# A two-mixer decoder trunk on one core: both mixers group by group, or the first for all groups and then the second

## The chip, the cores and the metric

The kernel runs on one core of a Trainium2 chip. The metric is the device time of one execution in microseconds (us). TensorE is called PE, VectorE DVE, ScalarE ACT, GpSimd POOL, and SyncE, which issues most transfers, SP.

## What is computed

The input is x, 2048 tokens of 1024 features in float32. There are two layers, each with RMS norm, a shift, scale and gate from a conditioning vector, and a residual:

```
h = rms_norm(x) * (1 + scale) + shift
u, v, z = split(h @ w_in)                    # first mixer, 3 x 2048 columns
y = gelu(u) * (w_s[causal] @ layer_norm(gelu(v)) + b_s) * silu(z)   # chunks of 128 tokens, 8 column groups
x1 = x + gate * (y @ w_out)
k, v = split(rms_norm(x1) * kv_norm @ w_kv)  # 2 heads of 64, k rotated
q, z = split((rms_norm(x1) * (1 + scale) + shift) @ w_in_b)         # 16 heads of 64, q rotated
o = softmax(q k^T / 8, window of 128, a learned sink per head) v
out = rms_norm(x1 + gate * ((o * silu(z)) @ w_out_b)) * final_norm
```

Attention works on blocks of 128 queries against this block and the one before it.

## The kernel before

The tokens are cut into four groups of 512 (`group(i)`), and a group's 512 tokens are four chunks of 128. A group goes through both mixers before the next begins; group 0 is written out and the others run in a loop (`groups`), on every engine.

**Numbers in halves.** All large products are made from a rounded high part and a remainder: high x high, high x low, low x high, three matmuls for one (`split3`, L1329 to L1331). For weights ACT rounds (`hi`, L615) and POOL subtracts (`lo`, L508); for activations ACT rounds and DVE subtracts.

**Units and pieces.** The weights stream from HBM in units of 4 x 128 rows by 512 columns, into two buffers in turn; each unit arrives as two halves. A group has 44 units: 8 for v (`U_V`), 16 for u and z in eight slabs (`U_UZ`), 8 for the first output projection (`U_AO`), 4 for q, 4 for z, 4 for the second output projection (`U_BO`). A unit is eight pieces of six matmuls with 512 columns. `piece_done` counts pieces, and SP loads the unit after next into a buffer when its pieces are done.

**First mixer.** v is projected and its statistics taken; then each slab projects u and z, DVE forms `vs`, PE does the spatial matmuls (L1472), DVE gates (L1090 to L1115). Then y is split (`y_rest`) and projected. In group 0 DVE also makes the rotary tables (`table`, 17 operations on 128x512) between the y remainders, ACT takes their sines, and they go through HBM.

**Second mixer.** x1 is normalised and turned by PE (`x1_transposes`), copied, multiplied out to K and V, and the modulated `hb` is made by DVE and split. q is rotated: ACT copies a bank with its halves swapped (L660, four instructions), DVE multiplies by cosine and sine and adds (`rope`, L1006 to L1009), ACT rounds (L673, L674), DVE takes the remainder (L1019, L1020). The order is swap 0, swap 1, out 0, swap 2, out 1 and so on (`Q_BEFORE`). Attention is 16 steps, each four heads of one block:

```python
FILLERS = [4, 3, 2] + [2] * 4 + [3] * 9
```

is the number of projection pieces that PE does in each step; four more stand ahead (`AHEAD`). A step: logits (L1583, into two banks that all steps share); DVE masks and takes the maximum (L1245 to L1258); ACT exponentials (L855); DVE adds the sink, takes the reciprocal (L1267, L1269); POOL scales (L573); PE transposes (L1592, one step later, into bank 6); ACT and DVE split (L849, L1263); POOL makes the masked copy (L567); PE multiplies with V (L1604, three steps later, into bank 7); ACT and DVE combine it (L867, L1275). When a tile of o is whole, DVE gates it (L1033). Then come the output projection, the residual (`residual`, L1147 and L1151), the last norm (L1317) and the store. The next group's x is scaled, turned (L1359) and split beside the output projection.

The order on every queue is written out by hand: an engine that waits holds up all that stands behind it.

## Time and profile before

| | |
|---|---|
| three runs | 2602.76, 2607.14, 2607.95 us |
| median | 2607.14 us |
| profiled execution, span from first to last instruction | 2608.2 us |
| busy: PE, DVE, POOL, ACT | 90%, 55%, 46%, 41% |
| transfers | 250 MB, mean 96 GB/s |

The span is that of one profiled execution. No time of it outside the span is given; it lies within 0.3 us of the slowest run. PE's busy time counts overlapping matmuls once, and a busy PE need not run at its full clock; the granted clock is given as a share of 2.4 GHz, in which 0.5 is 1.2 GHz.

### The profile page before, as it was taken

How to read it: one execution, taken by the hardware profiler on the slowest of the kernel's cores; microseconds unless marked ns; L12 is line 12 of the kernel's file. 1: busy time of each engine (PE TensorE's matmuls, PEld its weight loads, DVE VectorE, ACT ScalarE, POOL GpSimd, SP SyncE). 2: the span in 40 equal slices, each digit the busy share in tenths (PEclk: the TensorE clock that was granted, in tenths of full speed). 3: DMA queues.
4: the chain of work that ended last, by engine and by line, in shares of the span. 5: the costliest groups of instructions: out<-in, count | busy, mean ns of one | idle time of the engine just before them, and what ended most of it. 6: DMA issues, size and time to landing. Idle time of an engine off the chain costs nothing.

```text
span 2608.2 us, 31861 instructions
## 1 busy us (share of the span) xinstructions
PE 2341.7 (90%) x10725; PEld 1929.0 (74%) x10725; DVE 1443.3 (55%) x1885; ACT 1057.6 (41%) x1979; POOL 1187.1 (46%) x597
## 2 busy tenths in 40 slices
PE   4999997878899999887889999987898999998787
PEld 3878885656688888776678888876677888886566
DVE  6645477678533443568651444267854254436784
ACT  3222232655442223365453222347544222236552
POOL 3344343255554444435645444524654444452564
PEclk9999998988899999998999999998999999998998
DMA  7642232211232224211223222421133322322112
GB/s 268 238 172 89 88 129 85 74 36 41 105 129 89 89 88 138 89 49 33 97 74 129 91 88 88 136 73 49 41 105 106 97 89 88 129 97 65 41 33 89
DMA packets 151955, 250.04 MB, mean 96 GB/s; under 512 B 9408, under 2 KB 80160, under 8 KB 151712
## 3 DMA queue, kind: packets, MB, share of 16 engines
q1 hardware_dynamic: 147104, 234.94, 27.3%
q10 hardware_dynamic: 4736, 13.67, 1.3%
q8 instruction: 60, 0.98, 0.1%
...
## 4 chain that ended last, share of the span: by engine, by line
issue 28%; PE 21%; POOL 17%; DVE 16%; ACT 8%; DVEq 6%; DMA 2%; POOLq 2%; ACTq 0%; SPq 0%
POOL w_lo L508 16%; PE ps L1329 6%; PE ps L1330 6%; PE ps L1331 6%; DVEq L1247 4%; ACT pp L855 3%; DVE es L1267 3%; ACT zb L660 2%; DVE mx L1252 2%; DVE ob L1033 1%; DVE negm L1255 1%; DVE zb L1006 1%; DVEq L1008 1%; POOLq L515 1%; DVE ps L1245 1%
## 5 line engine op out<-in xcount | busy, mean ns | idle before, releaser
L508 POOL TENSOR_TENSOR w_lo<-w_raw,w_hi 128x1024 fp32r<-128x1024 f32 x352 | 879.5, 2511 | 1061.6 <-ACT w_hi L615 1061.1
L615 ACT ACTIVATE w_hi<-w_raw 128x1024 fp32r<-128x1024 f32 x352 | 370.1, 1059 | 798.3 <-DMA w_raw<-in_a_w_in 577.4
L1329 PE MATMUL ps<-hb,w_hi 128*128 128x512 f32 x512 | 213.7, 417 | 23.1 <-DVE zb L1006 22.1
L567 POOL TENSOR_TENSOR pt<-pt,keep 128x1024 fp32r<-128x1024 f32 x64 | 152.3, 2380 | 174.1 <-DVE pt L1263 174.1
L1329 PE MATMUL ps<-w_hi,y_hl 128*128 128x512 f32 x512 | 202.8, 396 | 22.5 <-POOL w_lo L508 22.5
L1101 DVE SCALAR_TENSOR_TENSOR wz<-wz,ps 128x512 f32<-128x512 f32 x64 | 43.6, 687 | 315.8 <-ACT wz L733 315.8
L1330 PE MATMUL ps<-hb,w_hi 128*128 128x512 f32 x512 | 209.8, 410 | 0.0
L1331 PE MATMUL ps<-hb,w_lo 128*128 128x512 f32 x512 | 208.7, 408 | 0.0
L1329 PE MATMUL ps<-h_low,w_hi 128*128 128x512 f32 x512 | 202.6, 396 | 6.3 <-ACT vy L705 3.6
L1330 PE MATMUL ps<-w_lo,y_hl 128*128 128x512 f32 x512 | 201.3, 393 | 0.0
L1331 PE MATMUL ps<-w_hi,y_hl 128*128 128x512 f32 x512 | 201.0, 393 | 0.0
L1331 PE MATMUL ps<-h_low,w_lo 128*128 128x512 f32 x512 | 200.1, 391 | 0.0
L1330 PE MATMUL ps<-h_low,w_hi 128*128 128x512 f32 x512 | 200.0, 391 | 0.0
L1329 PE MATMUL ps<-h_high,w_hi 128*128 128x512 f32 x512 | 199.2, 389 | 0.0
L1330 PE MATMUL ps<-h_high,w_hi 128*128 128x512 f32 x512 | 199.2, 389 | 0.0
L1331 PE MATMUL ps<-h_high,w_lo 128*128 128x512 f32 x512 | 199.2, 389 | 0.0
L1123 DVE TENSOR_TENSOR y_hl<-vy,y_hl 128x512 fp32r<-128x512 f32 x64 | 77.5, 1269 | 169.3 <-ACT y_hl L745 169.2
L855 ACT ACTIVATE pp<-ps,negm 128x128 f32<-128x128 f32 x256 | 90.7, 366 | 188.7 <-DVE negm L1255 188.7
...
L1329 PEld LDWEIGHTS ps<-hb,w_hi 128*128 128x128 f32 x512 | 103.2, 202 | 49.7 <-DVE zb L1006 28.6
L1592 PE MATMUL ps<-ident,pp 128*128 128x128 f32 x256 | 44.7, 303 | 99.7 <-DVE pt L1263 99.6
L1329 PEld LDWEIGHTS ps<-w_hi,y_hl 128*128 128x128 f32 x512 | 97.3, 190 | 44.5 <-issue 20.5
...
## 6 DMA issues: line engine op xcount, KB each, us to landing
w_raw<-in_a_w_in SPq DMA_DIRECT2D x256, 256.0 KB, 2.8
...
```

Source lines behind the costliest of these rows:

```text
L508: g.tensor_tensor(wlo[p][:, rows_], raw[p][:, rows_], whi[p][:, rows_].bitcast(F32), ALU.subtract).then_inc(w_lo, 1)
L567: g.tensor_tensor(pt[:, k % 2, 2:4].rearrange("p a (h q) -> p (a h) q", h=4), pt[:, k % 2, 0:2].bitcast(F32).rearrange("p a (h q) -> p (a ...
L615: s.activation(whi[p][:, rows_], raw[p][:, rows_], ACT.Copy).then_inc(w_hi, 1)
L660: last = s.activation(zb[32 * q:32 * q + 32, 2 * (n % 2), :], ps[o:o + 32, 512 * b:512 * b + 512], ACT.Copy)
L855: last = s.activation(pp[:, st % 2, h, :], ps[:, 2048 + 256 * h + P:2048 + 256 * h + 2 * P], ACT.Exp, bias=negm[:, st % 2, h:h + 1], scale ...
L1123: v.tensor_tensor(y[:, t % 4, 1, :], vy[:, T * t:T * t + T], y[:, t % 4, 0, :].bitcast(F32), ALU.subtract).then_inc(y_lo, 1)
L1247: dve.drain()
L1252: v.tensor_reduce(mx[:, slot, :], both[:, :, P:2 * P], AXIS_X, ALU.max)
L1267: v.tensor_tensor(es[:, slot, :], es[:, slot, :], psum_[:, slot, :], ALU.add)
L1329: t_.matmul(dst, stat[0], mov[0], start=start, stop=False)
L1330: t_.matmul(dst, stat[0], mov[1], start=False, stop=False)
L1331: return t_.matmul(dst, stat[1], mov[0], start=False, stop=stop)
```

## The change

The four groups go through the first mixer one after the other; the next group's x is now turned beside the last unit of the first output projection. Each group's x1 is stored in HBM (`x1_kept`); it is scaled and turned by PE one tile after each slab of the next group, copied by ACT and stored as well (`x1_turned`). The rotary tables are made after slabs 0 to 3 of group 0.

Then a second phase runs the second mixer of all groups. Its weight units stand in one list: K/V, q and z of the first eight heads for group 0; then, for each group i, q and z of the other eight heads, the output projection of group i-1, and K/V, q and z of the first eight heads of group i+1; last the output projection of group 3. The 416 pieces of the 52 units are dealt out over slots: 8 slots without attention, 64 slots with one attention step each, 8 slots at the end. The probabilities are transposed after the first piece of the next slot and multiplied with V after its fourth; the transposes and the products now share bank 6. DVE gates o in every step, and the gated, split output goes through HBM (`oz_kept`) except for group 3. K/V's input is scaled from the stored turned tile by ACT and its remainder taken by DVE (`xk_round`, `xk_rest`); `hb` is made by ACT from the same tile during the K/V unit, whose weights are now an ordinary unit without kv_norm in them. Weights of a later unit are split on ACT and POOL two pieces after their buffer is free. All loops are written out. The residual keeps its product in the PSUM bank.

The core of the diff, by engine:

```diff
-UNITS = 44
-PIECES = 8 * UNITS
-U_V, U_UZ, U_AO, U_Q, U_Z, U_BO = 0, 8, 24, 32, 36, 40
-STEPS = 16
+U_V, U_UZ, U_AO, A_UNITS = 0, 8, 24, 32
+FIRST_B = A_UNITS * NG
+def b_order():
+    units, starts = [], []
+    def kv_q0_z0(g):
+        units.append(("kv", g, 0, 0))
+        for kind in "qz":
+            for ku in range(2):
+                units.append((kind, g, 0, ku))
+    starts.append(0)
+    kv_q0_z0(0)
+    for i in range(NG):
+        starts.append(len(units))
+        for kind in "qz":
+            for ku in range(2):
+                units.append((kind, i, 1, ku))
+        if i >= 1:
+            for n in range(2):
+                for ku in range(2):
+                    units.append(("b", i - 1, n, ku))
+        if i < NG - 1:
+            kv_q0_z0(i + 1)
+    starts.append(len(units))
+    for ku in range(2):
+        for n in range(2):
+            units.append(("b", NG - 1, n, ku))
+    return units, starts + [len(units)]
+PRO_SLOTS, STEPS, TAIL_SLOTS = 8, 16, 8
+def b_slots():
+    slots = []
+    for it, count in enumerate([PRO_SLOTS] + [STEPS] * NG + [TAIL_SLOTS]):
+        first, n = 8 * B_STARTS[it], 8 * (B_STARTS[it + 1] - B_STARTS[it])
+        for s in range(count):
+            slots.append(range(first + n * s // count, first + n * (s + 1) // count))
+    return slots
+def by_halves(u):
+    if u < FIRST_B:
+        return u % 2 == 0 and u % A_UNITS != U_AO + 6
+    kind, g, n, ku = B_UNITS[u - FIRST_B]
+    return kind == "kv" or ku == 0 or (kind == "b" and n == 1 and g < NG - 1)
+def freed(u, hh):
+    return 4 + 4 * hh if by_halves(u) else 8
+AFTER_FREE = 2
+def weights_at(pc):
+    found = []
+    for u in range(FIRST_B + 2, UNITS):
+        for hh in range(2):
+            if 8 * (u - 2 - FIRST_B) + freed(u - 2, hh) - 1 + AFTER_FREE == pc:
+                found.append((u, hh))
+    return found
...
+        x1d = nc.dram_tensor("x1_kept", [NG, P, NC, D], F32).ap()
+        xtd = nc.dram_tensor("x1_turned", [NG, KT, P, T], F32).ap()
+        ozd = nc.dram_tensor("oz_kept", [NG - 1, KT, P, 2, T], F32).ap()
...
 sync
+            def keep_turned(i, kt):
+                sp.wait_ge(t1_copied, at("t1_copied", i, kt + 1))
+                sp.dma_start(xtd[i, kt], xst[:, kt % 2, :]).then_inc(xt_out[kt % 2], 16)
...
+                for g in range(GROUPS + 1):
+                    unit(first + U_UZ + 2 * g)
+                    unit(first + U_UZ + 2 * g + 1)
+                    if i >= 1 and g >= 1:
+                        keep_turned(i - 1, g - 1)
...
+            def load_oz(g, half):
+                done = B_AT[("z", g + 1, 1, half)]
+                sp.wait_ge(piece_done, b_pieces(8 * done + 8))
+                for n in range(2):
+                    sp.wait_ge(oz_out[n], 16 * (4 * g + 2 * half + 2))
+                sp.dma_start(r[:, 4 * half:4 * half + 4].bitcast(F32),
+                             ozd[g, 4 * half:4 * half + 4].rearrange("k p a t -> p k a t")).then_inc(oz_in[half], 16)
...
 gpsimd
+            for s, slot in enumerate(SLOTS):
+                a = s - PRO_SLOTS
+                for k, pc in enumerate(slot):
+                    tasks(pc)
+                    if k == 0:
+                        if 0 <= a - 1 < ATT:
+                            mask(a - 1)
+                        if 0 <= a < ATT:
+                            normalise(a)
...
 scalar
+            def hb_round(g, kt):
+                act.wait_ge(piece_done, b_pieces(8 * B_AT[("kv", g, 0, 0)] + kt + 1))
...
+                for dst_ in (hfx[:, kt % 2, :], r[:, kt, 0, :]):
+                    last = s_.activation(dst_, xin[:, kt, :], ACT.Identity, bias=sb_[:, kt:kt + 1],
+                                         scale=gb[:, kt:kt + 1])
...
+            def tasks(pc):
+                kind, g, n, ku, k = unit_of(pc)
...
+                kind2, g2, n2, ku2, k2 = unit_of(pc - 2)
+                if kind2 == "q" and ku2 == 1 and k2 % 2 == 1:
+                    m = 4 * n2 + k2 // 2
+                    act.wait_ge(roped, at("roped", g2, m + 1))
...
+                    s_.activation(qs[0:64, 2 * m, :], whole[0:64, :], ACT.Copy)
+                    s_.activation(qs[64:P, 2 * m + 1, :], whole[64:P, :], ACT.Copy).then_inc(q_hi, 1)
+                if kind == "q" and ku == 1 and k % 2 == 1:
...
+                    swap_from(m % 4, zb[2 * (m % 2)], swapped)
...
+                for u, hh in weights_at(pc):
+                    hi(u, (hh,))
+                if kind == "kv":
+                    hb_round(g, k)
...
 vector
+                for g in range(GROUPS - 1):
+                    uz_group(g)
+                    if i == 0 and g < NG:
+                        table(g)
+                    if g == 2 and i < NG - 1:
+                        x_scale(i + 1)
...
+            def residual(x_, b, cnk, n, gate, read):
+                dve.drain()
+                v.tensor_tensor(bank(b), bank(b), gate[:, 512 * n:512 * n + 512], ALU.mult)
+                dve.drain()
+                v.tensor_tensor(x_[:, cnk, 512 * n:512 * n + 512], x_[:, cnk, 512 * n:512 * n + 512], bank(b),
+                                ALU.add).then_inc(read, 1)
...
+                for k, pc in enumerate(slot):
+                    tasks(pc)
+                    if k == 0:
+                        if 0 <= a < ATT:
+                            dve.wait_ge(sink_exp, a + 1)
+                            v.tensor_tensor(es[:, at_, :], es[:, at_, :], psum_[:, at_, :], ALU.add)
+                            dve.drain()
+                            v.reciprocal(rden[:, at_, :], es[:, at_, :]).then_inc(r_ready, 1)
...
+                    if k == min(3, len(slot) - 1) and 0 <= a - 1 < ATT:
...
+                        v.tensor_tensor(obt[0:64], high[:, :, 0, :], ot[0:64], ALU.add)
+                        v.tensor_tensor(obt[64:P], high[:, :, 1, :], ot[64:P], ALU.add)
+                        dve.drain()
+                        gated = zg[:, f0:f0 + 2, P * blk:P * blk + P]
+                        v.scalar_tensor_tensor(gated, obt[:], 0.5, gated, ALU.mult, ALU.mult).then_inc(o_done, 1)
...
 tensor
-                for f in range(AHEAD):
-                    filler(f)
-                for st in range(STEPS):
-                    f = AHEAD + sum(FILLERS[:st])
-                    logits(st)
-                    filler(f)
-                    if st >= 3:
-                        values(st - 3)
-                    filler(f + 1)
-                    for k in range(2, FILLERS[st]):
-                        filler(f + k)
-                    if st >= 1:
-                        p_transposes(st - 1)
+            for s, slot in enumerate(SLOTS):
+                a = s - PRO_SLOTS
+                if 0 <= a < ATT:
+                    logits(a)
+                for k, pc in enumerate(slot):
+                    b_piece(pc)
+                    kind, g, _, _, kk = unit_of(pc - 2)
+                    if kind == "kv" and kk == 7:
+                        k_transposes(g)
+                    if 24 <= pc < 24 + KT:
+                        x1_transposes(NG - 1, pc - 24, 4 + pc % 2)
+                    if k == 0 and 0 <= a - 1 < ATT:
+                        p_transposes(a - 1)
+                    if k == min(3, len(slot) - 1) and 0 <= a - 1 < ATT:
+                        values(a - 1)
```

## Rows read from the trace of the kernel before

**Rows 1.** The page, engines over the whole span: busy us (share) xinstructions.

```profile
PE 2341.7 (90%) x10725; PEld 1929.0 (74%) x10725; DVE 1443.3 (55%) x1885; ACT 1057.6 (41%) x1979; POOL 1187.1 (46%) x597
```

**Rows 2.** Stretches: busy us of each engine, then granted clock, DMA share, GB/s.

```profile
54.30:460.50 406.20, 383.01 (x1729) 316.20 (x1728) 239.19 (x278) 115.23 (x146) 162.26 (x68) 0.97 0.39 132
...
723.40:1091.00 367.60, 364.72 (x1677) 303.50 (x1676) 143.70 (x171) 115.67 (x148) 172.52 (x78) 1.00 0.33 106
1091.00:1351.00 260.00, 213.64 (x986) 173.70 (x984) 186.76 (x266) 147.32 (x345) 121.64 (x64) 0.91 0.19 61
...
2349.00:2608.20 259.20, 205.07 (x954) 164.19 (x952) 180.23 (x264) 136.84 (x331) 119.66 (x68) 0.92 0.17 57
```

**Rows 3.** Stretches of group 1's second mixer; columns as before.

```profile
1150.30:1293.30 143.00, 116.71 (x521) 93.25 (x520) 116.03 (x179) 81.70 (x239) 81.40 (x43) 0.89 0.15 47
```

**Rows 4.** Waits of PE, 1091 to 1351 us: total, times, longest.

```profile
PE ps L1592 <- DVE pt L1263: 23.4, 9, 5.1
...
PE ps L1329 <- DVE zb L1006: 5.8, 4, 2.0
```

**Rows 5.** Timeline of PE, dense matmuls: start us, us, instruction.

```profile
1348.11 0.39 PE L1329 MATMUL ps<-w_hi,oz 128*128 128x512 f32 x1
...
1350.15 0.39 PE L1329 MATMUL ps<-w_hi,oz 128*128 128x512 f32 x1
```

**Rows 6.** Timeline inside an attention step, all engines.

```profile
1234.70 2.40 POOL L567 TENSOR_TENSOR pt<-pt,keep 128x1024 fp32r<-128x1024 f32 x1 [2.88 <-DVE pt L1263]
...
1235.28 0.60 PE L1592 MATMUL ps<-ident,pp 128*128 128x128 f32 x4
...
1235.44 1.68 DVE L1267 TENSOR_TENSOR es<-es,psum__137 128x4 f32<-128x4 f32 x1 [0.81 <-ACT es L860]
...
1236.66 0.39 PE L1329 MATMUL ps<-hb,w_hi 128*128 128x512 f32 x1
```

**Rows 7.** DVE groups, one row a shape: busy us, mean ns | idle before.

```profile
L1009 DVE TENSOR_TENSOR zb<-zb 128x512 f32<-128x512 f32 x36 | 41.0, 1140 | 2.7
...
L1020 DVE TENSOR_TENSOR qs<-zb,qs 64x512 fp32r<-64x512 f32 x32 | 38.8, 1214 | 0.4
...
L1007 DVE TENSOR_TENSOR zb<-zb,cs 128x512 f32<-128x512 f32 x36 | 29.8, 828 | 0.0
...
L1182 DVE TENSOR_TENSOR kvn<-xt,kvn 128x512 fp32r<-128x512 f32 x32 | 29.2, 953 | 10.1 <-ACT kvn L791 10.1
...
L1006 DVE TENSOR_TENSOR zb<-ps,cs 128x512 f32<-128x512 f32 x36 | 24.9, 692 | 51.8 <-ACT zb L660 50.5 <-issue 1.0
...
L1019 DVE TENSOR_TENSOR qs<-zb,qs 64x512 fp32r<-64x512 f32 x32 | 24.2, 757 | 2.9
L1317 DVE SCALAR_TENSOR_TENSOR x<-x,r,fn 128x1024 f32<-128x1024 f32 x16 | 22.5, 1417 | 25.0 <-POOL r L516 25.0
```

**Rows 8.** ACT groups, columns as in the group above.

```profile
L615 ACT ACTIVATE w_hi<-w_raw 128x1024 fp32r<-128x1024 f32 x352 | 370.1, 1059 | 798.3 <-DMA w_raw<-in_a_w_in 577.4 <-DMA w_raw<-in_a_w_out 190.6 <-DMA w_raw<-in_b_w_out 24.0
...
L660 ACT ACTIVATE zb<-ps 32x512 f32<-32x512 f32 x144 | 84.9, 589 | 2.4 <-PE ps L1528 0.2
...
L673 ACT ACTIVATE qs<-zb 64x512 fp32r<-64x512 f32 x32 | 20.2, 631 | 5.7 <-DVE zb L1009 5.2
```

**Rows 9.** POOL groups, columns the same.

```profile
L508 POOL TENSOR_TENSOR w_lo<-w_raw,w_hi 128x1024 fp32r<-128x1024 f32 x352 | 879.5, 2511 | 1061.6 <-ACT w_hi L615 1061.1 <-issue 0.2
```

**Rows 10.** PE groups, columns the same.

```profile
L1359 PE MATMUL ps<-ident,xs 128*128 128x128 f32 x128 | 24.5, 364 | 25.3 <-DVE bt L1147 22.4 <-ACT h_low L638 2.8
```

**Rows 11.** Waits of PE in group 0's first mixer.

```profile
PE ps L1329 <- POOL w_lo L508: 19.8, 2, 13.9
```

**Rows 12.** Timeline of DVE, half of one rotary table.

```profile
412.23 0.43 DVE L978 TENSOR_SCALAR tab<-tab 128x512 f32<-128x512 f32 x1
...
416.55 0.43 DVE L992 TENSOR_SCALAR tabo<-tab 128x512 f32<-128x512 f32 x1
```

**Rows 13.** Timeline of PE, the last matmul of the kernel.

```profile
2597.95 0.39 PE L1331 MATMUL ps<-w_hi,oz 128*128 128x512 f32 x1
```

1867 lines of the change are left out of this document (922 added, 945 removed).

## Prediction

> **What bounds the kernel now.** I read the engines' totals first. PE is busy 90% of the span [rows 1], and no other engine is over 55%. That share hides two kinds of stretch. Cut at the first matmul of each stage, the span is 54.3 us of start, a first mixer of 406.2 us (group 0), three of about 367.6, and four second mixers that share the rest: 2608.2 - 54.3 - 406.2 - 3 x 367.6 = 1044.9 us, about 261 each [rows 2]. In a first mixer PE is busy for 364.7 of 367.6 us at a granted clock of 1.00. In a second mixer it is busy 213.6 of 260.0 at 0.91, and DVE is busy 186.8, which is 72%.
>
> The price of PE's work comes from starts, not from durations, since matmuls overlap: nine 512-column matmuls start in 2.04 us, so one costs 0.227 us [rows 5]. A piece (six of them) is 1.37 us, a unit (eight pieces) 10.9. An attention step adds four transposes and eight logits matmuls, 1.38 us from 1235.28 to 1236.66 [rows 6], and four value matmuls, 0.91: 2.3 us. The first mixer is thus at its PE floor (32 units are 349 us, the spatial matmuls make up most of the rest). The second is not: 12 units 131, 16 steps 37, K/V 11, transposes about 7, together 186 of 261 us.
>
> What holds it is in the sixteen steps: 143.0 us, 8.9 us a step, DVE busy 116.0 (81%), PE clock 0.89 [rows 3]. Step work of PE is 2.3 plus 2.25 projection pieces, 5.4 us. The longest wait of PE in group 1's whole second mixer is that of the probability transposes for DVE's split of the step before, 23.4 us in 9 waits, and 5.8 us go to rope, ahead of the steps [rows 4]. So a second mixer is a cross-engine chain with DVE nearly full, and pieces between its links are too few.
>
> **The change part by part.** First mixer, groups 1 to 3: same units. PE now also turns the next x (24.5/4 = 6.1 us by its busy time [rows 10], which overlaps; I take 4) and the kept x1 (the same number of transposes, 4). Their copies on ACT and the scale on DVE lie in a stage where ACT is busy 115.7 and DVE 143.7 of 367.6 us [rows 2]; if that cover were gone they would cost about 2 us for each of eight tiles. That gives 375, 375, and 371 for group 3, which turns no next x. SP now waits for each turned tile between weight loads, behind it stands the next unit's load; it waits only for a copy that is due early in the slab, so nothing is charged.
>
> Group 0: 19.8 us of waiting for w_lo go [rows 11], whose root is ACT standing in its queue for the tables that DVE makes. The tables move between DVE's slab work. One table is two halves of 16 operations in all; one half takes 4.75 us without company [rows 12], so about 10, up to 14 where POOL is in the way. DVE is free for 61% of a first mixer [rows 2], 14 us of a slab's 23.6, but the table stands between one slab's gating and the next one's `vs`, for which PE's spatial matmuls wait; in slab 2 the scaling of the next x (four operations on 128x1024, 1.4 each like L1317 [rows 7]) is added. I charge 2 us for three slabs and 9 for slab 2, 15 in all, and take 5 off for the clock that the old wait had lowered (0.97 in the row). 406.2 - 19.8 - 5 + 15 + 4 = 400. The four: 1521. If the tables hide, 1506; if each comes in full, 1545.
>
> Second mixers: the work is now 416 pieces and 64 steps: 40 pieces in 8 slots before the first step, then 72, 104, 104 and 64 pieces over 16 steps each, then 32 pieces in 8 slots. PE's floor for the four is 72 x 1.37 + 37 = 136, 180, 180, 125: 620 us (old steps had 36 pieces for 16). Start: 55 + 4 for the last x1 transposes; tail: 44.
>
> DVE's load. The old steps' 116.0 us hold four ropes of 0.69 + 0.83 + 1.14 = 2.66, four q remainders of 1.97, eight z gates of 0.69 (they read PSUM, as rope's first operation does), and four output gates with remainders, 6.5 [rows 7]. 85.5 are left, 5.3 a step. New in each step is the gating of 128x256 from SBUF, which no row shows; between 0.35 (half of L1006's 512 columns) and 0.95 (L1182), I take 0.65: 6.0 a step, 95 for 16. Around them per group: eight ropes and K's 24, q remainders 16, z gates 5.5, output remainders 5.5, second residual 8 x 1.44 (now both operations read PSUM) 11.5, final scale 4 x 1.42, xk remainders 8 x 0.95, hb remainders 5.5, K/V about 6. Put where they fall, the four iterations hold 162, 179, 179 and 142 us: 662. Gone from DVE there are x1's normalisation, the whole hb (ACT makes it from the stored tile), half the K/V splits, and both x stages. So DVE has more than PE, 662 against 620. The engines are level, and the time is set by how well the queues mesh.
>
> Two ways to size it. By fill: at the 81% of the old steps, 662/0.81 = 817. By stalls on PE, which are 620 plus:
> - Rope. ACT's order is now: q high parts of column m-1 (which wait for its rope), then the swap of m. A column is 4 x 0.59 swap [rows 8] + 2.66 rope + 2 x 0.63 = 6.3 us in series against 2.74 for PE's two pieces. The fourth bank is read 3 x 6.3 + 2.4 + 0.7 = 22 us after the first is full; PE wants it after nine pieces and one to two steps, 15 us. At least 7, and with a step's DVE work in between up to 20. I take 14, seven times: 98. Queued behind ACT's wait are the exponentials and w_hi, and PE's next logits and weights wait for those.
> - K/V units: two activations per piece on ACT for hb, 1.3 of 1.37 us, beside a step's 3 us: 7, three times, 21.
> - Mask: after the transposes come a copy on ACT (0.6, as L673) [rows 8], DVE's remainder (0.7, as L1006) [rows 7] and POOL's 2.4 [rows 6], 3.9 us with the hand-overs against three pieces, 4.1. It fits unless POOL has just begun a 2.5 us weight half [rows 9]; 0.5 a step, 32.
>
> That is 771. I take 800. Start with one rope stage unhidden: 71. Tail: PE's last matmul stands 10 us before the old end [rows 13], the same chain follows here, and the last step drains in it: 57. Extra transfers (x1 and its turned copy out and in, the gated output of three groups) are hidden: the queues are used 17 to 19% in these stretches [rows 2]. ACT takes up new weights two pieces after the buffer is free, 2.7 us, and may stand a microsecond for them; that is within the 30 between the two ways. SP passes these stores and loads between weight loads; behind a 2 MB load one weight half comes late by some 6 us, which has twelve pieces of slack.
>
> Sum: 54 + 1521 + 71 + 800 + 57 = 2503 against the profiled 2608.2. The runs' median lies 1 us under that span: about 2502.
>
> A rule is weighed here. In a step, DVE's 4-element sum of `es` takes 1.68 us and ends at 1237.12, with POOL's mask at 1237.10 [rows 6]. The Trainium skill (SBUF — State Buffer, Who interferes with whom) says that a DVE instruction with two SBUF inputs is fully blocked while a GpSimd instruction reads SBUF. The trace agrees. By that rule the new gating and xk operations wait too, and POOL's share in iterations 1 and 2 (an old step's 3.4, which is 81.4 less 11 weight halves over 16, so 16 x 3.4 + 26 halves x 2.5 = 120 of some 210 us) is no higher than the 57% of the old steps [rows 3], so the mean durations used above carry over. At a full mask wait for every new gating, 2.4 instead of 0.65, it would be 64 x 1.75 = 112 us more, 2614.
>
> **The rivals.** (1) The chain hides and PE sets the time: mask and K/V stalls alone, 620 + 53 = 673 for the slots, start 60, tail 54: 2362, up to 2430 with half the rope stalls. For: slots of 4.5 to 6.5 pieces where 2.25 stood, and PE reached 1.00 wherever it was fed. Against: DVE's 662 alone, and waits in fixed order.
> (2) Slower: the in-order coupling lets DVE fill only as it does over a whole old second mixer, 72% [rows 2]: 662/0.72 = 919, and 54 + 1521 + 71 + 919 + 57 = 2622. It decides from 905 us in the slots, a fill of 73%, or 14.1 us a slot. For: the rope chain in series, in which ACT, then DVE, then PE stand. Against: old stretches at 72% held stages with no step to run beside them (normalisation, output projection); here they overlap.
> (3) No change: the gain is exactly eaten, the slots at 895 to 905.
>
> **How the numbers follow.** 0.2% (5 us) is about what a measurement of this kernel can tell from no change. Forecast, slots 740 to 890, 2440 to 2590: 0.64. Rival 1: 0.20. Rival 2, with what lies between it and the forecast: 0.14. Rival 3: 0.02. Range: 2395 (between rival 1's two values) to 2605; about 0.1 is left out on each side. Faster 0.86, same 0.02, slower 0.12.
>
> **What would show it.** First mixers of 371 to 376 us, group 0 near 400 with waits of spatial matmuls for `vs` and no 13.9 us wait for w_lo. Sixteen-step stretches near 175, 226, 226 and 173 us, DVE above 75% busy, PE's clock above 0.91 except at q stages; PE waiting for rope's first product at z's first pieces, 10 us and more at a time; transposes waiting for DVE's gating or for exponentials. Wrong if the slots are nearly PE's floor with few rope waits (rival 1), if DVE is under 73% busy there and ACT stands for rope (rival 2), or if weights arrive late behind SP's new waits.

## The result and the profile after

The change makes the kernel slower. The kernel after takes 2634.7 us (median of four runs, 2633.7 to 2638.2), the kernel before beside it 2606.0 (2602.8 to 2608.0): ratio 1.0118, 95% interval 1.0100 to 1.0136. Forecast were 2502 us, 2395 to 2605 and a faster kernel: the time lies outside the range and on the other side. Below, a run's time is the median of its fast executions, since one execution of one kernel (`e16_rest_later`) fell in a slower state and took 2988.7 us.

The engine totals of the kernel after hardly differ from those of before [rows 1]:

```profile
PE 2323.3 (88%) x10725; PEld 1919.2 (73%) x10725; DVE 1436.3 (55%) x1900; ACT 1076.8 (41%) x2018; POOL 1171.0 (44%) x573
```

Stretches of the kernel after, cut where its stages begin: four first mixers, the start of the second phase up to the first logits, the four iterations of sixteen slots, and the tail. The columns are those of [rows 2].

```profile
54.30:459.00 404.70, 394.37 (x1809) 326.22 (x1808) 244.13 (x287) 135.16 (x176) 165.41 (x68) 1.00 0.43 145
459.00:828.00 369.00, 368.27 (x1720) 307.41 (x1719) 147.91 (x173) 125.57 (x167) 163.61 (x70) 1.00 0.35 116
...
1568.00:1651.50 83.50, 53.81 (x228) 43.26 (x229) 31.27 (x42) 45.87 (x75) 20.74 (x10) 0.82 0.22 70
1651.50:1867.70 216.20, 154.32 (x734) 125.36 (x733) 154.25 (x242) 125.79 (x314) 100.88 (x49) 0.90 0.21 71
1867.70:2133.80 266.10, 205.28 (x934) 167.63 (x933) 182.67 (x271) 139.42 (x334) 125.49 (x66) 0.89 0.31 109
2133.80:2400.00 266.20, 210.43 (x934) 172.21 (x933) 184.53 (x268) 139.43 (x334) 125.54 (x66) 0.87 0.31 109
2400.00:2575.70 175.70, 138.61 (x647) 109.33 (x645) 135.93 (x211) 89.91 (x253) 99.83 (x51) 0.93 0.31 108
2575.70:2632.90 57.20, 45.32 (x194) 37.02 (x194) 30.21 (x34) 14.53 (x24) 23.58 (x21) 0.91 0.31 111
```

The first phase is full: PE is busy 368 of 369 us, at a clock of 1.00. The deviation lies behind it. The 64 slots take 216.2 + 266.1 + 266.2 + 175.7 = 924.2 us where 800 were forecast, and DVE is busy 657.4 of them, 71%. The last iteration, which holds one rotary stage and no K/V unit, takes 175.7 us for the 173 of the forecast; the other three, with two rotary stages and a K/V unit each, take 40 us more than forecast apiece. PE's longest waits in the slots of the kernel after, and two of ACT's (time, number of waits, longest):

```profile
PE ps L1603 <- POOL pt L675: 101.8, 46, 7.0
PE ps L1596 <- DVE zg L1390: 68.0, 27, 11.1
PE ps L1399 <- DVE zb L1243: 15.5, 6, 5.4
PE ps L1399 <- DVE x L1114: 13.2, 8, 2.9
PE ps L1399 <- ACT vf L917: 11.3, 2, 5.7
```

```profile
...
ACT qs L931 <- DVE zb L1246: 64.8, 25, 4.3
...
ACT w_hi L717 <- DMA w_raw<-in_b_w_in: 26.7, 7, 9.3
```

PE seldom waits for the rope itself (15.5 us). It waits for the mask (L675, by the value products L1603) and for the gating (L1390, by the transposes L1596), which stand on POOL and DVE behind everything else. These names tell who was last, not why. So I sorted the slots: from each step's logits to the next, against PE's price as the prediction has it, 1.37 us a piece and 2.3 a step. A slot is called K/V if it holds a piece of a K/V unit, rotary if it or the four pieces ahead of it hold a piece of a q unit's second half (there the columns become ready), other if neither.

| 63 slots, us | rotary (23) | K/V (8) | other (32) |
|---|---|---|---|
| PE's price | 225.5 | 85.5 | 299.6 |
| kernel after | 412.4 | 148.5 | 351.3 |
| over the price | 186.8 | 63.0 | 51.7 |
| of this PE idle | 134.0 | 42.1 | 37.2 |
| PE busy beyond its price | 52.8 | 20.9 | 14.5 |
| mean granted clock | 0.83 | 0.84 | 0.98 |

The other slots run near the price: iteration 1's slots 4 to 8 take 10.7 to 12.0 us. The rotary ones do not: its slots 1 to 3 take 20.2, 18.4 and 25.0.

The excess is not all waiting. Slots 1 to 3 and then 4 to 8 of iteration 1, and around one wait in slot 15 (columns as above):

```profile
1878.40:1942.00 63.60, 41.89 (x170) 33.26 (x169) 42.66 (x59) 30.52 (x70) 26.07 (x12) 0.84 0.26 96
1942.00:2000.20 58.20, 56.31 (x273) 46.10 (x272) 38.75 (x64) 28.17 (x77) 37.08 (x18) 1.00 0.49 172
...
2122.70:2127.05 4.35, 0.02 (x2) 0.04 (x1) 0.68 (x1) 0.00 (x0) 4.35 (x3) 1.00 0.00 0
2127.40:2130.80 3.40, 3.40 (x10) 2.66 (x9) 1.09 (x3) 0.76 (x2) 0.50 (x1) 0.50 0.00 0
2131.00:2134.00 3.00, 3.00 (x16) 2.49 (x15) 0.69 (x1) 0.65 (x2) 0.00 (x0) 1.00 0.00 0
```

At a granted clock of 1.00 PE is busy 56.3 us for work whose price is 55.3; at 0.84 it is busy 41.9 for 34.3. In the third stretch PE stands and the clock is still at 1.00; in the fourth it is at 0.50 (1.2 GHz), and 128x512 matmuls that otherwise start 0.23 us apart start 0.43 apart; in the fifth it is back. So a wait of PE is paid twice here, once as idle time and once in the slower matmuls behind it. Over the 64 slots PE is busy 708.6 us for a price of 620 and idle 215.6.

### The profile page after: what moved, and what is told of

It is laid out like the page before. It is cut to its first block, busy times and chain, and to the rows that moved or that the text cites. A ratio compares the mean times of both kernels' runs of the same rounds, so it can differ in the third digit from the quotient of the medians.

```text
span 2632.9 us, 28491 instructions
## 1 busy us (share of the span) xinstructions
PE 2323.3 (88%) x10725; PEld 1919.2 (73%) x10725; DVE 1436.3 (55%) x1900; ACT 1076.8 (41%) x2018; POOL 1171.0 (44%) x573
## 4 chain that ended last, share of the span: by engine, by line
PE 63%; DVE 14%; ACT 7%; DVEq 5%; DMA 4%; issue 4%; POOL 3%; SPq 0%; POOLq 0%; ACTq 0%
PE ps L1399 19%; PE ps L1400 19%; PE ps L1401 19%; POOL pt L675 2%; ACT zb L872 2%; PE ps L1549 2%; DVEq L1351 2%; DMA w_raw<-in_b_w_in 1%; DVEq L1245 1%; DVE zb L1246 1%; ACT pp L994 1%; DVE mx L1356 1%; DVE zb L1243 1%; DVEq L1388 1%; DVE es L1371 1%
## 5 line engine op out<-in xcount | busy, mean ns | idle before, releaser
L1399 PE MATMUL ps<-h,w_hi 128*128 128x512 f32 x1024 | 401.9, 392 | 0.0
L1401 PE MATMUL ps<-h,w_lo 128*128 128x512 f32 x1024 | 398.8, 389 | 0.0
L1400 PE MATMUL ps<-h,w_hi 128*128 128x512 f32 x1024 | 398.6, 389 | 0.0
L1399 PE MATMUL ps<-r,w_hi 128*128 128x512 f32 x512 | 224.4, 438 | 46.3 <-ACT vf L917 25.8
L675 POOL TENSOR_TENSOR pt<-pt,keep 128x1024 fp32r<-128x1024 f32 x64 | 156.8, 2451 | 224.8 <-DVE pt L1365 224.8
L1401 PEld LDWEIGHTS ps<-h,w_lo 128*128 128x128 f32 x1024 | 192.3, 188 | 40.6
L1399 PEld LDWEIGHTS ps<-h,w_hi 128*128 128x128 f32 x1024 | 192.4, 188 | 39.4 <-POOL w_lo L618 0.4
L1400 PEld LDWEIGHTS ps<-h,w_hi 128*128 128x128 f32 x1024 | 192.5, 188 | 39.3
L1400 PE MATMUL ps<-r,w_hi 128*128 128x512 f32 x512 | 215.8, 421 | 0.0
L1401 PE MATMUL ps<-r,w_lo 128*128 128x512 f32 x512 | 213.4, 417 | 0.0
L1399 PE MATMUL ps<-w_hi,h 128*128 128x512 f32 x512 | 201.2, 393 | 1.9 <-POOL w_lo L618 1.9
L1401 PE MATMUL ps<-w_hi,h 128*128 128x512 f32 x512 | 200.0, 391 | 0.0
L1400 PE MATMUL ps<-w_lo,h 128*128 128x512 f32 x512 | 200.0, 391 | 0.0
L1129 DVE BATCH_NORM_STATS2 stats<-vy 128x6 f32<-128x512 f32 x64 | 42.6, 689 | 231.5 <-ACT vy L774 231.4
L1399 PEld LDWEIGHTS ps<-r,w_hi 128*128 128x128 f32 x512 | 108.0, 211 | 70.1 <-issue 26.4
```

Source lines behind the costliest of these rows:

```text
L675: g.tensor_tensor(pt[:, 2:4].rearrange("p a (h q) -> p (a h) q", h=4), pt[:, 0:2].bitcast(F32).rearrange("p a (h q) -> p (a h) q", h=4), k ...
L1129: v.bn_stats(stats[:, cnk, j, :], src[:, :, cnk, :])
L1399: t_.matmul(dst_, stat[0], mov[0], start=start, stop=False)
L1400: t_.matmul(dst_, stat[0], mov[1], start=False, stop=False)
L1401: return t_.matmul(dst_, stat[1], mov[0], start=False, stop=stop)
```

## The experiments

Eighteen runs. Each ratio is to the kernel before on the same chip, with its 95% interval. The theories of the first four runs are A, the rope chain in series on ACT; B, DVE has too much work in whatever order; C, weights come late; D, the bank shared by transposes and products is freed late.

### The rope chain on ACT: the swap first, and the same made worse in the kernel before

`e1_swap_first`, on the kernel after: ACT swaps column m before it rounds column m-1, which waits for DVE's rope.

```diff
-                if kind2 == "q" and ku2 == 1 and k2 % 2 == 1:
-                    ...   # wait for rope m-1, round it to qs
                 if kind == "q" and ku == 1 and k % 2 == 1:
                     ...
                     swap_from(m % 4, zb[2 * (m % 2)], swapped)
+                if kind2 == "q" and ku2 == 1 and k2 % 2 == 1:
+                    ...   # wait for rope m-1, round it to qs
```

> The changed kernel with one order turned round on ScalarE: the half-swap of q column m stands ahead of the rounding of column m-1, which waits for VectorE's rope of m-1. Same instructions, same load. Theory A (the rope chain in series: swap 2.4, rope 2.7, rounding 1.3 us per column, with an attention step's work caught behind it): a column drops from 6.3 to about 3.7 us, seven stages in the slots win 7 to 10 us each and the one ahead of them 8: 2550 to 2575 us. Theory B (VectorE simply has too much work for the slots, in whatever order): no more than 10 us, 2625 to 2635. Theory C (weights come late) and theory D (the bank that transposes and value products share is freed late) expect no change either.

Measured: 2599.3 us, ratio 0.9982 (0.9968 to 0.9996), 35 us less than the kernel after. The direction is theory A's, the gain about half of the 60 to 85 us that it expected. The excess of the rotary slots fell from 186.8 to 153.9, the start of the second phase shortened as well (the first logits came 9.7 us earlier), and the other slots stayed (57.2).

The timeline of the kernel after shows the series that this cuts. In brackets is the idle time before an instruction, and who ended it. First DVE, then ACT in the same stretch:

```profile
1897.79 0.69 DVE L1246 TENSOR_TENSOR zb<-zb,zb 128x512 f32<-128x512 f32 x1
1902.30 0.69 DVE L1243 TENSOR_TENSOR zb<-ps,cs 128x512 f32<-128x512 f32 x1 [3.82 <-ACT zb L872]
...
1905.87 0.70 DVE L1349 COPY_PREDICATED ps<-prev,ps 128x512 f32<-128x512 uint32 x1
...
1907.74 0.68 DVE L1365 TENSOR_TENSOR pt<-ps,pt 128x512 fp32r<-128x512 f32 x1
```

```profile
1898.52 0.63 ACT L931 ACTIVATE qs<-zb 64x512 fp32r<-64x512 f32 x1 [3.83 <-DVE zb L1246]
1899.16 0.63 ACT L932 ACTIVATE qs<-zb 64x512 fp32r<-64x512 f32 x1
1899.81 2.39 ACT L872 ACTIVATE zb<-ps 32x512 f32<-32x512 f32 x4
```

ACT stands 3.83 us for DVE's rope, then DVE 3.82 us for ACT's swap: each idles while the other works. DVE's softmax (L1349) and its remainder of the probabilities (L1365) stand in line behind, so the wait reaches PE under the mask's name.

`b1_serial_before` gives the kernel before the same serial order.

```diff
-Q_BEFORE = (("in", 0), ("in", 1), ("out", 0), ("in", 2), ("out", 1), ("in", 3), ("out", 2), ("out", 3))
+Q_BEFORE = (("in", 0), ("out", 0), ("in", 1), ("out", 1), ("in", 2), ("out", 2), ("in", 3), ("out", 3))
```

> The kernel before, with the four q columns ahead of its attention steps in the changed kernel's order (swap 0, rounding 0, swap 1, rounding 1 and so on). Theory A: a column goes from 3.7 to about 6 us, so three columns in each of four groups cost 5 to 10 us a group, 20 to 40 us: 2628 to 2648. Theory B: VectorE has little to do there, no change beyond 5 us.

Measured: 2637.9 us, ratio 1.0127 (1.0105 to 1.0148): 33 us more, as theory A expected. That one order costs as much in either kernel, so the change, beside all else, had given up an order on ACT worth as much as its whole loss against the kernel before.

### The shared bank: two tries, no effect

`e2_bank_release`, on the kernel after: the bank counts as free once DVE has read it (`obt`), not once the output is gated.

```diff
-                        v.tensor_tensor(obt[64:P], high[:, :, 1, :], ot[64:P], ALU.add)
+                        v.tensor_tensor(obt[64:P], high[:, :, 1, :], ot[64:P], ALU.add).then_inc(o_read, 1)
...
-                    pe.wait_ge(o_done, a)
+                    pe.wait_ge(o_read, a)
```

> The changed kernel with a separate semaphore that frees the shared bank after the two additions that read it, instead of after the gating behind them. Theory D (transposes wait for the shared bank; 72 us of TensorE's waits in the slots name the gating): the gating's 0.4 to 2.4 us leave that chain in the steps where TensorE waits, 15 to 40 us off, 2595 to 2620. Theory A: the bank is late because the additions themselves stand behind the rope chain; 5 to 12 us, 2623 to 2630.

Measured: 2638.8 us, ratio 1.0132 (1.0112 to 1.0151): no gain, outside both theories' ranges. Theory D in this form falls. `e9_two_banks` takes the sharing away altogether.

```diff
-                if a >= 1:
+                if a >= 1 and product_bank(a - 1) == 6:
                     pe.wait_ge(o_done, a)
...
-                t_.matmul(bank(6), vst[:, blk, kh, :], pt[:, 0, :], start=True, stop=False)
+                if b == 7:
+                    pe.wait_ge(o_done, a)
+                    pe.wait_ge(k_read, turned[0])
+                t_.matmul(bank(b), vst[:, blk, kh, :], pt[:, 0, :], start=True, stop=False)
```

> One edit to the kernel after: a step's value products go to PSUM bank 7, which else only K's transposes use (two or three steps around those keep bank 6), so the next step's transposes in bank 6 no longer wait for VectorE to gate the outputs of the step before; the value products wait for it instead. Theory H (a ring): transposes, ScalarE's copy, VectorE's remainder, GpSimd's mask, value products, ScalarE's and VectorE's read of the result and the gating, then the next transposes, each waits for the one before, and the ring goes round once a step; that is why the mask first gave 35 us back of the waits for the mask and lost 29 to those for zg, and why value products put later made 100 us more of the latter. With two banks the ring is cut: the waits of transposes for zg (72 us) fall below 20, the value products still wait for the mask, and the time falls by 20 to 60 us, to 2575 to 2615. Rival B (VectorE has too much to do, and whatever waits for it takes the wait): the waits move to the value products and the time stays within 8 us of 2634.

Measured: 2636.9 us, ratio 1.0134 (1.0117 to 1.0151). The transposes' wait indeed fell from 68 to 5.4 us; the value products took it over. PE's waits in the slots of this kernel ("issue" is a wait that the profile puts down to nothing):

```profile
PE ps L1615 <- issue: 124.8, 43, 8.6
PE ps L1406 <- DVE zb L1250: 25.9, 9, 7.5
PE ps L1615 <- POOL pt L682: 25.6, 4, 8.4
...
PE ps L1603 <- DVE zg L1397: 5.4, 2, 2.8
```

102 + 68 us became 150 + 5, and the time stayed: theory H, a ring through the bank, is refuted, and the rival expected this. What is late is late in either place.

### Weights and the 2 MB loads

`e3_weights_later`, on the kernel after: `AFTER_FREE = 4` in place of 2.

> The changed kernel with weights taken up on ScalarE and GpSimd four pieces after their buffer is free instead of two. Theory C (ScalarE stands for weights that have not landed, 39 us of its waits in the slots, and holds up exponentials and swaps): 15 to 35 us faster, 2600 to 2620. Theories A, B and D: within 8 us, and possibly slower by up to 10 since GpSimd's half comes closer to the unit that needs it.

Measured: 2660.2 us, ratio 1.0214 (1.0194 to 1.0234), 26 us slower, more than any theory allowed. Theory C in that form falls: ACT's waits for the in-projection's weights fell from 26.7 to 6.6 us, and the time rose. PE waits for a weight in the slots of neither kernel; its waits for the gating rose from 68.0 to 86.8 us and the longest for the mask from 7.0 to 10.6. POOL's longest wait for a `w_hi`, with the mask behind it, rose from 13.5 to 18.7. That this is the way the time was lost was not tried. But one wait for weights is real. The kernel after, SP's issues at the start of iteration 1, then what ACT does with it:

```profile
1867.86 0.90 SPq L441 DMA_DIRECT2D w_raw<-in_b_w_in  x2
1868.93 0.37 SPq L473 DMA_DIRECT2D xin<-x_turned  x1
1869.34 0.58 SPq L544 DMA_DIRECT2D x<-x_kept  x1
1874.76 8.33 SPq L441 DMA_DIRECT2D w_raw<-in_b_w_in  x2
```

```profile
1885.91 1.06 ACT L717 ACTIVATE w_hi<-w_raw 128x1024 fp32r<-128x1024 f32 x1 [9.32 <-DMA w_raw<-in_b_w_in]
1886.99 0.60 ACT L988 ACTIVATE pt<-ps 128x512 fp32r<-128x512 f32 x1
```

The weight half issued at 1874.76, behind two 2 MB loads, takes 11.1 us to land and comes 9.3 us after ACT is ready for it, and the copy of the probabilities is the next thing on ACT. `e6_x_split` issues the same loads in 512 KB parts, one at every third piece.

```diff
-                        load_xin(g + 1)
-                        sp.dma_start(x1[:], x1d[g - 1]).then_inc(xr_in, 16)
+                        parts += [(xin_part, g, q) for q in range(4)]
+                        parts += [(x1_part, g, q) for q in range(4)]
...
+                    if parts and (pc - slots_first(s)) % 3 == 2:
+                        part, pg, q = parts.pop(0)
+                        part(pg, q)
```

> One edit to the kernel after: the 2 MB loads of a group's turned x and of its kept x1, which SyncE issues whole at the first slot of each iteration, are issued in four parts of 512 KB, one at every third piece, so that weights are never behind more than one part. Same bytes, same buffers. Theory F (transfer order): ScalarE stood 9.84 us for a weight half behind such loads at the start of iterations 1 and 2 (26.7 us of waits in all for the in-projection's weights), and the first slots of these iterations took 20 us instead of 12; then the waits of ScalarE for weights fall to under 8 us and the time by 10 to 25 us, to 2610 to 2625. Rival (those slots are long for the rotary columns, and the load's wait lies beside them): no more than 5 us.

Measured: 2628.0 us, ratio 1.0103 (1.0086 to 1.0120), some 4 to 7 us less, which its interval does not part from that of the kernel after, and short of the 10 to 25 of theory F. In the trace the wait is lifted: the same half lands in 4.4 us, and ACT's waits for these weights fell from 26.7 to 9.2. Slot 1 of iteration 1 went from 20.2 to 13.3 us, slot 2 from 18.4 to 20.3, which gave a part back.

### GpSimd's order, and the place of the value products

`e5_mask_first`, on the kernel after:

```diff
                 for k, pc in enumerate(slot):
-                    tasks(pc)
                     if k == 0:
                         if 0 <= a - 1 < ATT:
                             mask(a - 1)
                         if 0 <= a < ATT:
                             normalise(a)
+                    tasks(pc)
```

> One edit to the kernel after: in each slot GpSimd takes the mask and the normalising ahead of the weight remainders (w_lo) of the slot's first piece; nothing else moves. In the trace of the kernel after, the value products wait 101.8 us for the masked probabilities from GpSimd (46 waits, up to 7.0). Theory E (queue order): part of it comes from w_lo standing ahead of the mask on GpSimd, which itself waits for ScalarE's w_hi (behind the exponentials, or behind a late weight): one w_lo took 9.2 us of waiting that way ahead of a mask. Then the waits of the value products for GpSimd fall by a third or more and the time by 8 to 25 us, to about 2612 to 2626. Rival (the mask is late because the probabilities come late from ScalarE and VectorE): 2.0 us a slot stays, and the time stays within 6 us of 2634.

Measured: 2620.9 us, ratio 1.0075 (1.0059 to 1.0092), 11 us less than the kernel after by the ratios, as theory E expected. The value products' waits for the mask fell from 101.8 to 66.3 us, but the transposes' waits for the gating rose from 68.0 to 101.2: here too most of the wait moved. The timeline of the kernel after shows what stood ahead of the mask, and PE behind it:

```profile
2122.25 2.35 POOL L618 TENSOR_TENSOR w_lo<-w_raw,w_hi 128x1024 fp32r<-128x1024 f32 x1 [8.74 <-ACT w_hi L717]
2124.55 2.35 POOL L675 TENSOR_TENSOR pt<-pt,keep 128x1024 fp32r<-128x1024 f32 x1
```

```profile
2127.05 0.47 PE L1603 MATMUL ps<-pt,vst 128*128 128x512 f32 x1 [4.33 <-POOL pt L675]
```

POOL idles 8.7 us for ACT, then makes a weight half for which PE does not wait anywhere in the slots, and only then the mask. With the mask first this slot (15 of iteration 1) takes 12.0 us instead of 18.1, and slot 10 12.3 instead of 18.2; slot 11, which ends the K/V unit, grew from 19.9 to 24.6 and gave a part back.

`e7_values_later`, on the kernel after: `min(3, len(slot) - 1)` becomes `min(5, ...)` on PE, ACT and DVE.

> One edit to the kernel after: a step's value products, and the two engines' work on their result, stand after the sixth piece of a slot instead of the fourth (slots of six and seven pieces, iterations 1 and 2; in the slots of five pieces they go from the fourth to the last, in those of four nothing changes). Theory G (the mask's chain is longer than the pieces laid over it): the waits for GpSimd's mask in iterations 1 and 2 nearly vanish (some 50 of the 102 us), and if the next step's wait for the bank (72 us for zg) does not grow by as much, the time falls by 10 to 30 us. Rival (the wait moves): the waits for zg grow by what the others lose, and the time is within 6 us of 2634 or longer; the gating of the outputs then comes behind two more pieces of work on VectorE and the next transposes wait for it.

Measured: 2656.9 us, ratio 1.0217 (1.0196 to 1.0238), 26 us slower. Its waits of PE in the slots:

```profile
PE ps L1596 <- DVE zg L1390: 171.4, 42, 13.1
PE ps L1603 <- POOL pt L675: 29.2, 22, 7.2
```

73 us less waiting for the mask, 103 more for the gating: the rival, at its longer end.

### Three edits together, and what is left

`e8_three` has `e1`, `e5` and `e6` together.

> Three edits to the kernel after together: the swapped partner ahead of the copy of the last column on ScalarE (alone 2599), the mask ahead of the weight remainders on GpSimd, and the 2 MB loads in four parts. If the rope chain, GpSimd's order and the order of transfers are separate causes, the gains add: 35 + about 15 + about 15, so 2565 to 2580. If they share the same slots (the q columns lie in the first slots of an iteration, where the 2 MB loads are too), the sum is less than half of the two new gains: 2585 to 2600. If neither of the new edits matters, 2599.

Measured: 2569.9 us, ratio 0.9886 (0.9869 to 0.9902): faster than the kernel before, and in the range for separate causes. By the ratios it is 25 us below `e1`, where the two edits gave 15 alone; the intervals of the five ratios do not part these two figures. So the gains add at the least. That each edit alone gave part of its gain back to a wait that another takes away would explain a surplus, but is not shown.

`e10_four` adds the second bank of `e9_two_banks` to it.

> The kernel with three edits (swapped partner first, mask first, 2 MB loads in four parts; 2569.9) and with the value products in bank 7 as well. The transposes of that kernel wait 83 us for VectorE's gating. Theory H: they fall below 20 and the time by 25 to 60 us, to 2510 to 2545, so that the change with four mended orders is 2 to 3% faster than the kernel before. Rival B: within 8 us of 2570.

Measured: 2567.3 us, ratio 0.9869 (0.9852 to 0.9885), not apart from `e8_three`: the rival again. `e14_later_two_banks` is `e10_four` with the value products at `min(5, ...)`.

> The kernel with four edits (swapped partner first, mask first, loads in parts, products in bank 7; 2567.3) with value products after the sixth piece of a slot instead of the fourth, as in the run that lost 26 us with one bank. There the next transposes waited 171 us for VectorE's gating; with two banks they need not. If that wait was the loss, the same edit now gains, by what the products no longer wait for the mask (119 us in all, half of it in iterations 1 and 2): 2540 to 2560. Rival B (VectorE's backlog, whatever is put where): the products find the next wait, the gating comes later into the next slot's softmax, and the time is 2567 to 2590.

Measured: 2570.1 us, ratio 0.9869 (0.9838 to 0.9900): no gain, as its rival expected, but no loss either. The 26 us of `e7_values_later` do not come back here; which of the four edits prevents them was not tried alone.

In `e10_four` a rotary slot is not a chain of idle engines any more. DVE in slots 2 and 3 of iteration 1; the logits of the next step begin at 1882.46, its softmax (L1378) at 1893.07, and PE waits 8.6 us for its products:

```profile
1881.81 0.69 DVE L1346 TENSOR_TENSOR qs<-zb,qs 64x512 fp32r<-64x512 f32 x1
1882.58 0.69 DVE L1272 TENSOR_TENSOR zb<-ps,cs 128x512 f32<-128x512 f32 x1
...
1887.07 0.43 DVE L1419 SCALAR_TENSOR_TENSOR zg<-obt,zg 128x256 f32<-128x256 f32 x1
1887.59 2.71 DVE L1345 TENSOR_TENSOR qs<-zb,qs 64x512 fp32r<-64x512 f32 x1
1890.31 2.73 DVE L1346 TENSOR_TENSOR qs<-zb,qs 64x512 fp32r<-64x512 f32 x1
1893.07 0.70 DVE L1378 COPY_PREDICATED ps<-prev,ps 128x512 f32<-128x512 uint32 x1
```

Not one of these lines has an idle time. But 4.1 us of them are not DVE's own work: the two remainders of 2.7 us, elsewhere 0.69 each, ran beside POOL's weight halves, which had themselves come late:

```profile
1887.11 5.38 POOL L647 TENSOR_TENSOR w_lo<-w_raw,w_hi 128x1024 fp32r<-128x1024 f32 x2 [8.66 <-ACT w_hi L746]
```

Four runs asked what that means. `e16_rest_later` moves the remainders (L1345, L1346) two pieces back, `unit_of(pc - 5)` for `unit_of(pc - 3)`, ahead of the rope that takes their buffer:

> The kernel with four edits (2567.3) and one more: VectorE makes the remainders of a rotary column (two of 64x512, 0.69 us each alone, 2.71 and 2.73 beside GpSimd's w_lo) two pieces later, ahead of the rope that takes their buffer again, so the remainders of a unit's last columns come behind the next step's softmax and not ahead of it. In that kernel's trace they stand between the logits (1882.46) and the softmax (1893.07) of a step whose products TensorE then waits 8.6 us for. Theory J (the order on VectorE: work that nothing waits for stands ahead of a step's softmax): the products' waits (119 us) fall by 20 to 40 and the time by 10 to 30 us, to 2537 to 2557. Theory B' (VectorE has too much work in those slots, in whatever order): within 6 us of 2567.

Measured: 2567.5 us (median of three), ratio 0.9863 (0.9841 to 0.9884): nothing. Theory J falls; the order inside DVE's queue is not it.

`e12_sum_on_pool` (on the kernel after) and `e15_five` (on `e10_four`) give the sum of the denominators and its reciprocal to POOL.

```diff
-                            dve.wait_ge(sink_exp, a + 1)
-                            v.tensor_tensor(es[:, at_, :], es[:, at_, :], psum_[:, at_, :], ALU.add)
-                            dve.drain()
-                            v.reciprocal(rden[:, at_, :], es[:, at_, :]).then_inc(r_ready, 1)
...
+                g.tensor_tensor(es[:, a % 2, :], es[:, a % 2, :], psum_[:, a % 2, :], ALU.add)
+                pool.drain()
+                g.tensor_tensor(rden[:, a % 2, :], es[:, a % 2, :], mone[:], ALU.pow)
```

> One edit to the kernel after: the sum of a step's denominators and its reciprocal (128x4 each) are made by GpSimd, right ahead of its normalising, instead of VectorE. In the kernel with two banks VectorE spends 1.35 us on the mean sum of 128x4, 86 us in 64 steps, because the sum stands beside GpSimd's mask of 2.34 us (one began 0.75 us after the mask did and ended with it), and waits 29 us more for ScalarE's exponential ahead of it; the reciprocal is 11 us. Theory B, now in the form that VectorE is behind by a local backlog (in the slots with rotary columns it is busy 0.88 to 0.93 of the time while TensorE waits, and a step's softmax begins 10 us after its logits): some 115 us of VectorE's time are taken away, and the time falls by 20 to 70 us, to 2565 to 2615. Rival H2 (a step's own chain from logits to value products is what takes the time, VectorE's backlog is not on it; the sum on GpSimd makes the chain no shorter, and GpSimd's queue longer): within 8 us of 2634.

> The kernel with four edits (2567.3) and the sum and reciprocal on GpSimd. Theory B: 20 to 70 us less, 2497 to 2547. Rival H2: within 8 us of 2567.

Measured: 2647.4 us, ratio 1.0171 (1.0139 to 1.0204), and 2576.8 us, ratio 0.9898 (0.9867 to 0.9930): by the medians 13 and 9 us slower than their bases, both outside either theory's range; the intervals of the second and its base overlap. DVE's busy time in the slots fell by 57.6 us in the first (657.4 to 599.8), POOL's rose by 84.6 (451.7 to 536.3); of this the power alone is 71.8:

```profile
L685 POOL TENSOR_TENSOR rden<-es,mone 128x4 f32<-128x4 f32 x64 | 71.8, 1123 | 9.1
```

Less work on DVE over the whole brought nothing in this form. The test is muddled: it took work from every slot and put a link of 1.1 us on POOL in its place, and which of the two shows was not tried apart. `e18_half_rope`, on `e10_four`, leaves out part of the rope, and so takes work away in the rotary stages alone; its result is not the kernel's.

```diff
                 v.tensor_tensor(whole[:], bank(b), cs[:, 0, :], ALU.mult).then_inc(read, 1)
-                v.tensor_tensor(other[:], other[:], cs[:, 1, :], ALU.mult)
                 dve.drain()
-                v.tensor_tensor(whole[:], whole[:], other[:], ALU.add).then_inc(done, 1)
+                v.tensor_tensor(whole[:, 0:32], whole[:, 0:32], other[:, 0:32], ALU.add).then_inc(done, 1)
```

> The kernel with four edits (2567.3), with part of the computation left out: of each rotary column's rope VectorE makes only the product with the cosines; the product with the sines is left out and the sum is cut to 32 of 512 columns (so q and k are rotated wrongly). In the slots that takes some 50 us of VectorE's busy time (31.1 for the product and 23.5 for the sum in 28 columns, less what the short sums cost), all of it in the slots with rotary columns; ScalarE, GpSimd, the transfers and TensorE do the same work. Theory B' (VectorE is the bound inside those slots, though not over the whole): the time falls by 35 to 60 us, to 2507 to 2532. Rival K (those slots wait for a chain over several engines, in which the rope is a link): each column shortens by 1.4 us, but only the first of a unit stands in the chain, and the time falls by 5 to 25 us. Neither: within 5 us.

Measured: 2529.8 us, ratio 0.9711 (0.9682 to 0.9741), 37.5 us less than `e10_four`: in the range of theory B', at its lower end, and above the 25 of rival K. The excess of the rotary slots fell from 134.7 to 102.0 us, that of the others stayed (39.9, now 42.7). Slots 1 to 3 of iteration 1, then the slots without rotary work, in `e10_four` and then in this kernel:

```profile
1852.50:1904.70 52.20, 38.18 (x170) 30.87 (x169) 44.36 (x59) 30.70 (x70) 26.18 (x12) 0.90 0.42 137
1904.70:1962.80 58.10, 56.23 (x274) 46.13 (x273) 42.35 (x64) 28.32 (x77) 37.15 (x18) 1.00 0.49 176
```

```profile
1849.00:1896.80 47.80, 37.97 (x170) 30.23 (x169) 38.98 (x55) 30.71 (x70) 26.15 (x12) 0.93 0.45 151
1896.80:1955.20 58.40, 56.23 (x274) 46.12 (x273) 42.64 (x64) 28.32 (x77) 37.12 (x18) 1.00 0.48 173
```

DVE's work in those three slots fell by 5.4 us and the slots by 4.4; the stretch after them, where PE is busy 97%, did not move. In `e10_four` DVE is busy 85% of slots 1 to 3; in the kernel after the same slots take 63.6 us and DVE is busy 42.7 of them, 67%. As long as the chain is in series the engines wait in turn, and when it is loosened DVE is nearly full.

But this run does not part load from chain. The rope is also a link between ACT's swap and ACT's rounding, and it became shorter. ACT's wait for it, in `e10_four` and then in this kernel:

```profile
ACT qs L970 <- DVE zb L1275: 28.0, 17, 3.9
```

```profile
ACT qs L970 <- DVE zb L1274: 7.7, 7, 2.5
```

Rival K counted only the first column of a unit as standing in the chain. A chain in which more columns stand could give the same gain, and DVE's share in slots 1 to 3 fell with the load, from 85 to 82%. What is shown is that a microsecond of rope costs some 0.8 us of time here (4.4 for 5.4), not by which way.

Three runs went for the start of the second phase and the K/V slots. `e11_squares_later` is `e8_three` with the last group's squares (and its root and scale) behind the first K/V unit:

> The kernel with three edits and one more, at the start of the second phase only: the squares, the scale and the root of the last group's x1 (4 x 1.06 us on ScalarE, four operations on VectorE) go behind the first K/V unit instead of ahead of it. The first K/V unit's copies of V come late there (TensorE waits 14.5 us for vf), which I put down to the squares and to the order on ScalarE. If so the first logits come 4 to 10 us earlier and the time is 2560 to 2566. Rival (the copies of V wait for the eight rounds of h on ScalarE, or the squares come to stand in the way of the transposes of x1): within 2 us of 2570, or longer.

`e17_h_later` is `e10_four` with the last four `hb_round` of each K/V unit four pieces later:

> The kernel with four edits (2567.3) and one more: of the eight rounds of h that stand on ScalarE and VectorE beside the eight pieces of the next group's K/V unit, the last four go four pieces later, behind ScalarE's copies of K and V. The slots with the K/V unit take 25.5 and 26.0 us there in iterations 1 and 2 (a slot of as many matmuls elsewhere 13), TensorE waits 10.0 and 11.2 us for the copy of V, and ScalarE has two activations of some 0.8 us a round ahead of it. If the rounds are what makes the copies late, the waits for V fall from 21 us to under 8 in iterations 1 and 2, the first logits come a few us earlier too, and the time falls by 10 to 22 us, to 2545 to 2557. Rival (the copies wait for VectorE's K work or the step's own exponentials): within 5 us of 2567.

Measured: 2567.9 us, ratio 0.9872 (0.9855 to 0.9890), and 2566.1 us, ratio 0.9864 (0.9844 to 0.9884). Both are the rival's: 2.0 and 1.2 us less than their bases, which cannot be told from nothing. `e19_six` has both on `e10_four`:

> A version meant to beat both kernels: the four edits, the last group's squares behind the first K/V unit, and the last four rounds of h behind the K/V copies. Alone the last two gave 2.0 and 1.2 us. If they add: 2562 to 2566; if they stand for the same wait at the start of the phase: 2565 to 2568.

Measured, five runs: 2568.2 us, ratio 0.9864 (0.9838 to 0.9889), 0.9 us above `e10_four`: the last two edits do not add. So the change with its orders mended is 1.1 to 1.6% faster than the kernel before, some 67 us below the kernel after, and `e8_three`, with three small edits, has nearly all of it.

## Why the prediction was wrong

**The first phase: right.** 54 + 1521 puts its end at 1575; it came at 1568. The first mixers took 404.7 us for 400, and 369, 371 and 369 for 375, 375 and 371. The tables were charged 15 us; the spatial products' waits for `vs` came to 8.4 in group 0 and 10.7 in all four.

**DVE's load and the tail: right.** 662 us were counted for DVE's work in the slots, 657.4 measured; the output gating took 0.74 us in the mean, where 0.65 was taken and POOL's whole mask, 2.4, feared. The tail is 57.2 for 57.

**The slots: the step that failed.** The sum had PE's price, 620, plus three stalls: "Rope. ... I take 14, seven times: 98", 21 for the K/V units and 32 for the mask. That is 771, and 924.2 was measured (800 were taken). Two parts of it failed.

The first is the size of the stalls. PE is idle 215.6 us for the 151 of the three terms: 134.0 in the rotary slots for 98, 42.1 in the K/V slots for 21, 37.2 in the others for 32.

The second is a term put at nothing. The price of 620 is that of matmuls 0.227 us apart, at a clock of 1.00, and PE was busy 708.6, 89 us more, at 0.87 to 0.93 (a small part of the 89 is the transposes of K, which the price leaves out). The rows at hand had it: an old second mixer is PE busy 213.6 us at 0.91 for a floor of 186 [rows 2], and the price of an old step was taken too low besides. It has 44 pieces for its 16 steps (the sum of `FILLERS`, and 44 x 6 + 16 x 16 = 520 of the 521 matmuls of [rows 3]), 2.75 a step and not 2.25. So the steps' price is 97 us, and PE was busy 116.7 for it.

The other way of sizing, a fill of 0.81, came from a stretch that already left out what surrounds the steps; the slots hold both, and the fill was 0.71.

**Why a rotary stage costs 27 us.** Over PE's price the rotary slots take 186.8 us, 27 for each of seven stages: 19 with PE idle, 8 with PE slow. The mechanism of the waits was in the prediction: ACT rounds a column, which waits for its rope, before it swaps the next. Its price was taken as what PE would wait for a bank. The runs show that PE hardly does (15.5 us); the price is paid by the attention step that shares the engines, whose softmax, remainder, mask and gating stand behind the rope on DVE and ACT. Of the 27, the serial order on ACT is about 5 (`e1`: 186.8 to 153.9, over seven) and the orders on POOL and SP 2 or 3 more (to 136.8 in `e8`). Half the rope is 5 of what is left (`e18`), as load on DVE or as a link of the chain. The other 15 no run explains.

**Claims of no cost that were wrong.** "behind a 2 MB load one weight half comes late by some 6 us, which has twelve pieces of slack": the slack is PE's, but ACT stands at the wait 9.3 us with the step's probabilities behind it. The lateness was well sized (11.1 us to land for 4.4 in `e6`); what lifting it is worth, 4 to 7 us, is not clear of the intervals. POOL's order was priced as a collision with a weight half of 2.5 us, 0.5 a step; not seen was that POOL idles for that half's `w_hi` (8.7 us in the row above) with the mask behind it.

**The start.** 71 us forecast, 83.5 measured. The serial chain is 10 of it (`e1`: the first logits 9.7 us earlier); moving the squares gave 2 (`e11`), and the rest is open.

**The rivals.** Rival 2 had the right size (919 us in the slots for 924.2, 2622 for 2634.7) and named the serial rope chain as its ground. It was given 0.14, because the old low fill was put down to stages that now overlap. My reading is that the overlap itself was the trouble: where work that fills DVE meets a chain that needs DVE at once, both wait. No run tested it as such, and rival 2's size came from an old mean fill, so that it fits so closely is in part luck.

**Open.** The K/V slots lose 60 to 72 us in every kernel with the change; `e17`, which aimed at that, took 4 off. How much of DVE's time in the rotary slots is its standing beside POOL, no run has parted. Nor is it shown why fewer microseconds on DVE, with the sum on POOL, end in a longer time; that the power in the chain does it would be argued from its 1.1 us alone. PE's wait for the residual (L1114, 13.2 us) was in no experiment.
